# Projection matmuls of the tokens dealt by whole groups of 24 in every second round of the delta stage

## The chip, the core and the metric

One core of one Trainium2 chip runs the whole program. The metric is device time in microseconds (us), the median of several executions. Engines: TensorE (PE) for matmuls and transposes, VectorE (DVE), ScalarE (ACT), GpSimd (POOL), and SyncE (SP), which issues the DMAs. All engines run their own instruction streams in order and meet at semaphores.

## What is computed

Two transformer blocks in a row, float32, 1024 tokens of width 1024. The change touches one stage of the first block, "delta". With `xn` the normalised input, this stage computes a gated delta rule over 4 heads of 128 channels in chunks of 64 tokens, from projections made by the stage before:

```
kk = k k^T ; m = strict_lower(beta * kk * decay)
sol = solve(I + m, [beta v, beta k exp(gc)])  -> u, w
for each chunk: v_new = u - w state
                o     = q_dec state + (q k^T * decay) v_new
                state = state * g_end + k_dec^T v_new
```

and beside it an independent product, `xn` times 2560 more columns of `w_in` (the gate of this branch and q, k, v, z of the next). That product is "the tokens' projection", and is needed only in the next stage.

## The kernel before, in words

The program is a row of phases (`open`, `delta`, `stick`, `trunk`, `ffn`) with a barrier of all engines between them. In each phase several stage objects have one generator per engine. `interleave` (L2538) goes through a list of numbers, the plan, and for each number lets that generator issue its instructions up to its next `yield`. Each engine walks the same plan, so the plan sets the order within every engine; semaphores set the rest. A generator's first call also issues what stands before its loop.

In `delta` there are four: `DeltaFront` (0), `DeltaBack` (1), `DeltaScan` (2) and `TokenProjection` (3). The plan of `delta_plan` (L1387) has 144 rounds: 4 opening rounds, then 14 rounds (s = 0 to 13) for each of t = 0 to 9. In tile period t the front works on tile t (t = 0 to 7), the back on tile t - 1 (t = 1 to 8), the scan on tile t - 2 (t = 2 to 9). A tile has 128 tokens.

- Front: transposes `q`, `k`, `v` in rounds 0, 1, 2 (L1013), decay rows in round 3 (L1032), transposes of `kn`, `kb`, `qn`, `qd` in 6 to 9 (L1013), products `kk` (L1053) and `qk_dot` (L1058) in 10 and 11. DVE makes `kn`, `kb` in round 5 (L927, L931). ACT copies `qd`'s transpose to `q_t` in round 9 (L883), for which it waits for `o_done` of the tile two before, as `q_t` has two buffers.
- Back: inverts a triangular matrix in five levels. Round 0: DVE makes `upper` (L1100, L1102), PE transposes it (L1141). For level 1 to 5: in the odd round s = 1, 3, 5, 7, 9 PE multiplies `bx` (L1150) and ACT copies it (L1085); in the next even round PE multiplies `update` (L1157 and L1158, 16 instructions) and DVE subtracts it into `lower` and `upper` (L1106, L1107), which the next `bx` waits for. Rounds 11 and 12: `u_dot` (L1164), `w_dot` (L1169), and DVE's copy of the latter (L1111).
- Scan: in rounds 1 and 7 `ws` and the first half of `o` (L1250, L1255), in rounds 3 and 9 `grow` and the second half of `o` (L1263, L1267, signalling `o_done`).
- Tokens' projection: 80 groups (10 chunks of 256 columns by 8 token tiles) of 24 matmuls (L1379 to L1381), each group in two steps of 12; so 160 steps and two that only store. Even groups are evicted by ACT (L1353), odd ones by DVE (L1365), in the second step. Weights are split into a rounded high and a low part by ACT (L1328) and DVE (L1333); the first chunk's split is issued by the generator's first call.

The opening rounds make the gates: 48 matmuls of a narrow projection (L993 to L995), its copies (L828), transposes (L1000), DVE's L893, then beta, exp and log on ACT (L832, L833, L836, L838), sums over tokens on PE (L1006) and four exponentials on ACT (L841, L842, L844). PE waits for these before the first transposes of the tile loop (L1013).

The semaphore between groups and evictions, and two accumulators:

```python
            if h == 0 and g >= 2:
                pe.wait_ge(self.copied[g % 2], g // 2)
```

Of the kernel before, what the change touches and what calls it, by code (L numbers as in the profile page):

```python
# [1386 lines left out]
def delta_plan(others):  # L1387


    plan, given = [], 0  # L1390
    rounds = Delta.OPENING + Delta.STEPS * (TT + 2)
    for i in range(rounds):
        t = (i - Delta.OPENING) // Delta.STEPS if i >= Delta.OPENING else -1
        if t < TT:
            plan.append(0)
        if 1 <= t <= TT:
            plan.append(1)
        if t >= 2:
            plan.append(2)
        want = others * (i + 1) // rounds  # L1400
        plan += [3] * (want - given)
        given = want
    return plan


# [3210 lines left out]
```

## Time and profile before

| | |
|---|---|
| median of 3 executions | 2792.08 us (2791.32 to 2796.21) |
| the profiled execution | 2794.54 us, its span 2792.8 us |
| PE busy | 2614.5 us, 94% |
| DVE, ACT, POOL busy | 1263.7, 938.2, 357.3 us |
| delta stage on PE | first matmul 180.28, first of the projection 196.08, last about 681 us |
| projection matmuls L1379, L1380, L1381 | 640 each |
| PE waits in the stage that the list of waits shows | L1141 for `upper`: 4.3 us in 7 times; L1379 for `w_lo`: 2.9 us once |

In the timeline each row is a run of one instruction: its start, its length with the tail that overlaps the next, and in brackets the engine's idle time before it and who ended it. PE's matmuls are pipelined, so the time a block holds PE is read from its start to the start of the next block. A float32 product of 4 heads shows as 8 instructions, a transpose of 4 heads as 4.

### The profile page before, as it was taken

The numbers are of one execution on the slowest core, as the hardware profiler recorded it, in microseconds if no ns is written. First come the engines' busy times: TensorE is split into PE (matmuls) and PEld (weight loads), VectorE is DVE, ScalarE is ACT, GpSimd is POOL, SyncE is SP. The second block draws the span as 40 slices with busy tenths as digits, with TensorE's granted clock in tenths as the row PEclk, the third lists the DMA queues.
The fourth block names the chain that finished last, engine by engine and source line by source line (L and its number), as shares of the span: only waits on it lengthen the run. The fifth ranks groups of instructions, "written<-read, shape, count | busy, mean of one in ns | idle before, by whom it ended". The sixth has DMA issues, their size and how long they took to land. (4 is left out here: it accounts for less than half of the span.)

```text
span 2792.8 us, 36573 instructions
## 1 busy us (share of the span) xinstructions
PE 2614.5 (94%) x14702; PEld 2246.8 (80%) x14702; DVE 1263.7 (45%) x1762; ACT 938.2 (34%) x1541; POOL 357.3 (13%) x450
## 2 busy tenths in 40 slices
PE   8969999997799998999996989979999999999999
PEld 6849999997688886888885777868888888878877
DVE  6523444442466754543225767554323332333452
ACT  4223222221455652122114767532111211222331
POOL 1002222220332310001012223011000000000000
PEclk9989999999799998999997999989999999999999
DMA  4222221112332215442343111063222222255532
GB/s 144 86 77 80 62 68 52 52 41 68 106 113 88 80 50 192 155 143 82 121 135 119 46 39 47 18 222 89 83 68 68 68 83 76 91 189 176 192 102 80
DMA packets 223712, 268.91 MB, mean 96 GB/s; under 512 B 55060, under 2 KB 154004, under 8 KB 223544
## 3 DMA queue, kind: packets, MB, share of 16 engines
q1 hardware_dynamic: 223544, 266.58, 30.0%
q8 instruction: 117, 1.92, 0.3%
q14 instruction: 51, 0.42, 0.0%
HBM read 187.21 MB, written 79.32 MB: 95 GB/s over the span
## 5 line engine op out<-in xcount | busy, mean ns | idle before, releaser
L3784 PE MATMUL ffn_up_acc<-mixed_hi,ffn_ring_hi 128*128 128x512 f32 x704 | 274.6, 390 | 2.5 <-DVE mixed_lo L2926 2.5
L3784 PE MATMUL ffn_up_acc<-mixed_hi,ffn_ring_lo 128*128 128x512 f32 x704 | 274.3, 390 | 0.0
L3784 PE MATMUL ffn_up_acc<-mixed_lo,ffn_ring_hi 128*128 128x512 f32 x704 | 274.2, 389 | 0.0
L1379 PE MATMUL delta_acc<-delta_w_hi,xn_hi 128*128 128x256 f32 x640 | 191.6, 299 | 2.9 <-DVE delta_w_lo L1333 2.9
L1381 PE MATMUL delta_acc<-delta_w_hi,xn_lo 128*128 128x256 f32 x640 | 181.3, 283 | 0.0
L1380 PE MATMUL delta_acc<-delta_w_lo,xn_hi 128*128 128x256 f32 x640 | 181.1, 283 | 0.0
L3784 PEld LDWEIGHTS ffn_up_acc<-mixed_hi,ffn_ring_hi 128*128 128x128 f32 x704 | 132.2, 188 | 30.0 <-issue 2.9
L3784 PEld LDWEIGHTS ffn_up_acc<-mixed_hi,ffn_ring_lo 128*128 128x128 f32 x704 | 132.2, 188 | 27.5
L3784 PEld LDWEIGHTS ffn_up_acc<-mixed_lo,ffn_ring_hi 128*128 128x128 f32 x704 | 132.3, 188 | 27.1
L4043 DVE TENSOR_TENSOR ffn_feed_lo<-ffn_feed_raw,ffn_feed_hi 128x1536 fp32r<-128x1536 f32 x44 | 77.4, 1759 | 146.2 <-ACT ffn_feed_hi L4035 146.2
L3754 DVE TENSOR_SCALAR ffn_conv<-ffn_padded,ffn_taps 128x1024 f32<-128x1024 f32 x22 | 16.6, 753 | 274.8 <-ACT ffn_padded L3735 274.8
L1379 PEld LDWEIGHTS delta_acc<-delta_w_hi,xn_hi 128*128 128x128 f32 x640 | 122.2, 191 | 8.9 <-issue 5.5
L426 DVE TENSOR_TENSOR_SCAN stick_keep<-stick_keep,stick_zero 128x127 f32<-128x127 f32 (+7 forms) x64 | 92.4, 1444 | 74.1 <-ACT stick_keep L378 73.4
L3735 ACT ACTIVATE ffn_padded<-ffn_up_acc 128x1024 f32<-128x1024 f32 x22 | 22.6, 1027 | 301.4 <-PE ffn_up_acc L3784 301.4
L1380 PEld LDWEIGHTS delta_acc<-delta_w_lo,xn_hi 128*128 128x128 f32 x640 | 122.2, 191 | 0.0
L1381 PEld LDWEIGHTS delta_acc<-delta_w_hi,xn_lo 128*128 128x128 f32 x640 | 121.9, 191 | 0.0
L4035 ACT ACTIVATE ffn_feed_hi<-ffn_feed_raw 128x1536 fp32r<-128x1536 f32 x44 | 65.4, 1487 | 158.9 <-PE ffn_up_acc L4111 158.9
L593 PE MATMUL stick_g_acc<-xn_hi,stick_g_hi 128*128 128x512 f32 x256 | 107.8, 421 | 9.3 <-DVE stick_g_lo L573 8.8
L4111 PE MATMUL ffn_up_acc<-ffn_feed_hi 128*128 128x512 f32 x352 | 108.7, 390 | 1.4 <-DVE ffn_emb L3897 1.4
L4111 PE MATMUL ffn_up_acc<-ffn_feed_hi,ffn_feed_lo 128*128 128x512 f32 x352 | 108.5, 390 | 0.0
L4111 PE MATMUL ffn_up_acc<-ffn_feed_lo,ffn_feed_hi 128*128 128x512 f32 x352 | 108.4, 390 | 0.0
L594 PE MATMUL stick_g_acc<-xn_lo,stick_g_hi 128*128 128x512 f32 x256 | 102.0, 399 | 0.0
(440 smaller groups left out, 6462.3 us busy)
## 6 DMA issues: line engine op xcount, KB each, us to landing
ffn_feed_raw<-in_w_down SPq DMA_DIRECT2D x44, 512.0 KB, 4.0
ffn_ring_raw<-in_w_gate SPq DMA_DIRECT2D x11, 1024.0 KB, 5.3
ffn_ring_raw<-in_w_up SPq DMA_DIRECT2D x11, 1024.0 KB, 5.8
scratch_act_t<-ffn_silu SPq DMA_DIRECT2D x22, 512.0 KB, 2.7
ffn_feed_raw<-scratch_act_t SPq DMA_DIRECT2D x44, 256.0 KB, 2.9
delta_w_raw<-in_w_in SPq DMA_DIRECT2D x20, 512.0 KB, 4.0
scratch_projected<-delta_out SPq DMA_DIRECT2D x80, 128.0 KB, 1.7
stick_g_raw<-in_w_in SPq DMA_DIRECT2D x16, 512.0 KB, 4.7
```

The source lines that it names most:

```text
L426: nc.vector.tensor_tensor_scan(back, back, self.zero[:].to_broadcast([P, n - 1]), 1.0, ALU.mult, ALU.add).then_inc(self.scanned, 1)
L593: nc.tensor.matmul(self.acc[:], w_hi, self.hi[:, k, cols], start=(k == 0), stop=False, skip_group_check=True)
L594: nc.tensor.matmul(self.acc[:], w_hi, self.lo[:, k, cols], start=False, stop=False, skip_group_check=True)
L1379: nc.tensor.matmul(acc, self.hi[:, k, tok], w_hi, start=(k == 0), stop=False, skip_group_check=True)
L1380: nc.tensor.matmul(acc, self.hi[:, k, tok], w_lo, start=False, stop=False, skip_group_check=True)
L1381: last = nc.tensor.matmul(acc, self.lo[:, k, tok], w_hi, start=False, stop=(k == self.kt - 1), skip_group_check=True)
L3735: nc.scalar.activation(self.padded[s][:, taps - 1:], self.acc[s][:, 0, :], ACT.Copy).then_inc(self.copied, 1)
L3754: nc.vector.tensor_scalar(self.conv[s][:], self.padded[s][:, 0:SEQ], self.taps_sb[:, f, 0:1], None, ALU.mult).then_inc(self.tapped, 1)
L3784: last = nc.tensor.matmul(self.acc[s][:, br, cols], weight[:, k, ch], part[:, k, cols], start=(k == 0 and first), stop=(k == 7 and weight ...
L4035: self.nc.scalar.activation(self.hi[s][:], self.raw[s][:], ACT.Copy).then_inc(self.hi_done[s], 1)
L4043: self.nc.vector.tensor_tensor(self.lo[s][:], self.raw[s][:], self.hi[s][:].bitcast(F32), ALU.subtract).then_inc(self.lo_done[s], 1)
L4111: last = nc.tensor.matmul(t.pairs[j][:, half, :], part, weight[:, HALF + half * HALF:HALF + (half + 1) * HALF], start=begins, stop=ends, s ...
```

## The change

```diff
@@ delta_plan @@
-        want = others * (i + 1) // rounds
-        plan += [3] * (want - given)
-        given = want
+        if i % 2 == Delta.OPENING % 2 or i == rounds - 1:
+            want = others * (i + 1) // rounds // 2 * 2
+            plan += [3] * (want - given)
+            given = want
```

`others` is 162 and `rounds` 144. Before, each round had one step of 12 matmuls, every eighth two. Now the steps stand in the even rounds of each tile period alone, two at a time (one group of 24), in some rounds four. The opening rounds 0 and 1 have none, round 2 has the first group, round 3 none. On PE the runs of projection matmuls without another instruction between them go from 121 to 68.

ACT in the opening rounds, from the copies of the narrow projection to the first exponentials (`delta_w_hi` is the high part of the projection's weights, `delta_out` the eviction of its first group). Before:

```order
L828 ACTIVATE delta_tok<-delta_back 8x512 x2
L1328 ACTIVATE delta_w_hi<-delta_w_raw 128x1024 x2
L832 ACT_TABLE_LOAD
L832 ACTIVATE delta_by_tile<-delta_ba 128x8x4
L833 ACT_TABLE_LOAD
L833 ACTIVATE delta_exp_a<-delta_a_row 128x4
L1353 ACTIVATE delta_out<-delta_acc 128x256
L836 ACTIVATE delta_expx<-delta_clip 128x32
L838 ACT_TABLE_LOAD
L838 ACTIVATE delta_rest<-delta_expx 128x32
L841 ACT_TABLE_LOAD
L841 ACTIVATE delta_by_tile<-delta_by_tile 128x8x4
```

And now:

```order
L828 ACTIVATE delta_tok<-delta_back 8x512 x2
L832 ACT_TABLE_LOAD
L832 ACTIVATE delta_by_tile<-delta_ba 128x8x4
L833 ACT_TABLE_LOAD
L833 ACTIVATE delta_exp_a<-delta_a_row 128x4
L836 ACTIVATE delta_expx<-delta_clip 128x32
L838 ACT_TABLE_LOAD
L838 ACTIVATE delta_rest<-delta_expx 128x32
L1328 ACTIVATE delta_w_hi<-delta_w_raw 128x1024 x2
L1353 ACTIVATE delta_out<-delta_acc 128x256
L841 ACT_TABLE_LOAD
L841 ACTIVATE delta_by_tile<-delta_by_tile 128x8x4
```

The split of the first weights and the first eviction move behind the logarithm.

PE in rounds 9 and 10 of a tile period with all three stages: `qd` transposed, `bx`, the two products of the scan, then what follows. Before:

```order
L1013 MATMUL delta_front<-ident,delta_qd 128x128 x4
L1150 MATMUL delta_back<-delta_lower,delta_bt 128x128 x4
L1263 MATMUL delta_ws<-delta_v_new,delta_k_end 128x128 x4
L1267 MATMUL delta_o_acc<-delta_v_new,delta_qk_t 64x128 x4
L1379 MATMUL delta_acc<-delta_w_hi,xn_hi 128x256
L1380 MATMUL delta_acc<-delta_w_lo,xn_hi 128x256
L1381 MATMUL delta_acc<-delta_w_hi,xn_lo 128x256
```

And now:

```order
L1013 MATMUL delta_front<-ident,delta_qd 128x128 x4
L1150 MATMUL delta_back<-delta_lower,delta_bt 128x128 x4
L1263 MATMUL delta_ws<-delta_v_new,delta_k_end 128x128 x4
L1267 MATMUL delta_o_acc<-delta_v_new,delta_qk_t 64x128 x4
L1053 MATMUL delta_front<-delta_t_sb 128x128 x4
L1157 MATMUL delta_back<-delta_bx,delta_upper 128x128
L1158 MATMUL delta_back<-delta_upper,delta_bx 128x128
```

Half a group stood between the scan's L1267 and the front's L1053; now L1053 and `update` follow directly.

DVE in rounds 3 to 6 of the same tile period (L1365 evicts a group, L927 makes `kn`). Before:

```order
L1237 TENSOR_TENSOR delta_state<-delta_faded,delta_ws 128x512
L1365 COPY delta_out<-delta_acc 128x256
L1106 TENSOR_TENSOR delta_lower<-delta_lower,delta_back 128x512
L1107 TENSOR_TENSOR delta_upper<-delta_upper,delta_back 128x512
L1333 TENSOR_TENSOR delta_w_lo<-delta_w_raw,delta_w_hi 128x1024
L927 TENSOR_TENSOR delta_kn<-delta_tok,delta_norm 128x512
L931 TENSOR_TENSOR delta_kb<-delta_kn,delta_by_tile 128x512
```

And now:

```order
L1237 TENSOR_TENSOR delta_state<-delta_faded,delta_ws 128x512
L1106 TENSOR_TENSOR delta_lower<-delta_lower,delta_back 128x512
L1107 TENSOR_TENSOR delta_upper<-delta_upper,delta_back 128x512
L1365 COPY delta_out<-delta_acc 128x256
L927 TENSOR_TENSOR delta_kn<-delta_tok,delta_norm 128x512
L931 TENSOR_TENSOR delta_kb<-delta_kn,delta_by_tile 128x512
L934 TENSOR_TENSOR delta_qn<-delta_tok,delta_norm 128x512
```

The eviction moves from before `lower` and `upper` to between them and `kn`, and the split of weights L1333 leaves this place.

## Rows read from the trace of the kernel before

**Rows 1.** Busy us by stretch: PE, PEld, DVE, ACT, POOL; then PEclk, DMA, GB/s

```profile
300.00:400.00 100.00, 99.39 (x838) 96.00 (x837) 44.76 (x64) 26.99 (x46) 22.92 (x19) 1.00 0.21 59
```

**Rows 2.** Timeline of PE, tile t = 4: start, length, instruction

```profile
400.19 1.05 PE L1032 MATMUL delta_front<-chunk_upto,delta_gb 128*128 128x128 f32 x8
...
401.32 1.13 PE L1150 MATMUL delta_back<-delta_lower,delta_bt 128*128 128x128 f32 x8
...
404.48 0.39 PE L1379 MATMUL delta_acc<-delta_w_hi,xn_hi 128*128 128x256 f32 x1
...
407.41 0.38 PE L1157 MATMUL delta_back<-delta_bx,delta_upper 128*128 128x128 f32 x2
...
409.11 0.36 PE L1379 MATMUL delta_acc<-delta_w_hi,xn_hi 128*128 128x256 f32 x1
...
410.82 1.13 PE L1150 MATMUL delta_back<-delta_lower,delta_bt 128*128 128x128 f32 x8
...
411.71 0.36 PE L1379 MATMUL delta_acc<-delta_w_hi,xn_hi 128*128 128x256 f32 x1
...
413.21 0.60 PE L1013 MATMUL delta_front<-ident,delta_kn 128*128 128x128 f32 x4
...
413.65 0.39 PE L1157 MATMUL delta_back<-delta_bx,delta_upper 128*128 128x128 f32 x2
```

**Rows 3.** Timeline of PE, tile t = 0

```profile
210.43 0.60 PE L1013 MATMUL delta_front<-ident,delta_xt 128*128 128x128 f32 x4
...
210.79 0.36 PE L1379 MATMUL delta_acc<-delta_w_hi,xn_hi 128*128 128x256 f32 x1
```

**Rows 4.** Timeline of ACT, s = 5 of t = 4

```profile
411.99 0.60 ACT L1085 ACTIVATE delta_bx<-delta_back 128x512 f32<-128x512 f32 x1 [5.35 <-PE delta_back L1150]
```

**Rows 5.** Timeline of PE and ACT, s = 9 of t = 4

```profile
428.85 0.39 PE L1379 MATMUL delta_acc<-delta_w_hi,xn_hi 128*128 128x256 f32 x1
...
429.02 0.60 ACT L883 ACTIVATE delta_q_t<-delta_front 128x512 f32<-128x512 f32 x1 [6.09 <-PE delta_o_acc L1267]
...
429.51 0.59 ACT L1085 ACTIVATE delta_bx<-delta_back 128x512 f32<-128x512 f32 x1
```

**Rows 6.** Timeline of PE, the first products of back in t = 1 and 5

```profile
237.19 0.66 PE L1141 MATMUL delta_back<-ident,delta_upper 128*128 128x128 f32 x4 [1.41 <-DVE delta_upper L1102]
...
443.63 0.66 PE L1141 MATMUL delta_back<-ident,delta_upper 128*128 128x128 f32 x4 [0.20 <-DVE delta_upper L1102]
```

**Rows 7.** Timeline of ACT, the opening rounds

```profile
193.73 1.99 ACT L1328 ACTIVATE delta_w_hi<-delta_w_raw 128x1024 fp32r<-128x1024 f32 x2
...
201.70 0.38 ACT L1353 ACTIVATE delta_out<-delta_acc 128x256 f32<-128x256 f32 x1 [0.85 <-PE delta_acc L1381]
...
203.52 0.23 ACT L838 ACTIVATE delta_rest<-delta_expx 128x32 f32<-128x32 f32 x1
...
203.76 1.28 ACT L841 ACT_TABLE_LOAD   x1
...
206.11 0.26 ACT L844 ACTIVATE delta_chunk_decay<-delta_o_acc 128x32 f32<-128x32 f32 x2
```

**Rows 8.** Timeline of PE, the opening rounds

```profile
196.08 0.39 PE L1379 MATMUL delta_acc<-delta_w_hi,xn_hi 128*128 128x256 f32 x1 [2.88 <-DVE delta_w_lo L1333]
...
197.79 1.02 PE L1000 MATMUL delta_ws<-ident,delta_tok 8*128 8x8 f32 x8
...
198.74 0.58 PE L1379 MATMUL delta_acc<-delta_w_hi,xn_hi 128*128 128x256 f32 x1
...
204.25 0.45 PE L1006 MATMUL delta_o_acc<-delta_g,chunk_upto 128*128 128x32 f32 x2
...
206.72 0.49 PE L1013 MATMUL delta_front<-ident,delta_xt 128*128 128x128 f32 x3
```

**Rows 9.** Busy time by stretches, columns as in rows 1

```profile
197.00:198.00 1.00, 1.00 (x9) 0.78 (x8) 0.16 (x1) 0.02 (x1) 0.00 (x0) 0.77 0.67 121
...
204.00:205.00 1.00, 0.98 (x9) 0.75 (x7) 0.19 (x1) 1.00 (x1) 0.00 (x0) 0.81 0.00 0
```

## The prediction

> **What bounds the kernel.** The stage is fenced by a barrier on either side, so only its own length counts. I read first the busy time by stretches: in the middle of the stage TensorE (PE) is busy 99.4% at the full clock (1.00, its 2.4 GHz level), VectorE (DVE) 45% and ScalarE (ACT) 27% [rows 1]. So the stage is as long as PE's work plus PE's waits; the change removes no matmul, and can only alter waits, the price of changing between kinds of matmul, and the clock.
>
> The list of waits shows few, since its ends are modelled; so I read the timeline and took start to start. Twelve projection matmuls take 1.50 (411.71 to 413.21), twenty-four 2.93 (404.48 to 407.41) [rows 2]: 1.43 for the second twelve, so entering a visit costs 0.08 us. But four transposes take 0.44 before another short product (413.21 to 413.65, [rows 2]) and 0.36 before a visit (210.43 to 210.79, [rows 3]): the short block gives the 0.08 back. **A visit of the projection is free at both ends**, and 121 visits becoming 68 (53 fewer, 1920 matmuls in both) earns nothing by itself.
>
> **What the new order takes away.** (a) Level 2's `bx` product (s = 3) now waits for DVE: L1032 took 1.13 before it (400.19 to 401.32) where eight such instructions take 0.89 (as 410.82 to 411.71) [rows 2]. A whole group ahead of it at s = 2 covers the missing 0.24: seven tiles (t = 1 to 7), -1.7 us. (b) At s = 4 a half group took 1.71 in place of 1.50 before `bx` (409.11 to 410.82), waiting for `upper` [rows 2]. Eleven places read so: s = 4 of seven tiles, and four in t = 8. All get 24 matmuls of cover: 11 times 0.21, -2.3. Together **-4.0**.
>
> **What it adds in the bare rounds.** The odd rounds have no projection now. Even to odd nothing is lost: 2.93 of cover stands where 1.50 did. Odd to even the chain is `bx` on PE, its copy on ACT (L1085), `update` on PE. The copy starts 1.17 after `bx` starts (410.82 to 411.99) and takes 0.60 [rows 2, 4]; the handover to PE is not shown for ACT, and I bound it by 0.05 and 0.15 and take 0.05 to 0.1: `update` can start 1.85 after `bx`. PE has 0.89 of `bx` itself, and then:
> - s = 5 to 6: only the four transposes of `kn`, 0.44: wait 0.5. On DVE the eviction L1365 of an odd group (s = 4 always has one in t = 1 to 7) now stands before `kn` (L927); group end + 0.2 + 0.33 + 0.69 + 0.1 = 1.3 lets the transposes begin 0.4 late, which lies inside the same 0.5. Seven tiles: 3.5.
> - t = 1 has no scan: s = 1 to 2 and s = 7 to 8 have 0.44 of transposes each (0.5 each), s = 3 to 4 has nothing (0.95). t = 8 has no front: s = 5 to 6, 0.95. Together 2.9.
> - s = 9 to 10, t = 2 to 7: ACT is in order, and `q_kept` (L883) ahead of the `bx` copy waits for the scan's `o_done` of this very round. The copy starts 0.66 after the scan leaves PE (428.85 to 429.51) and ends at 1.25 [rows 5]; `update` at 1.35, where PE has L1053, 0.89: 0.45 each, 2.7.
> - s = 1 to 2, 3 to 4 and 7 to 8 of t = 2 to 7: two scan products, some 1.9 to 2.1, cover 0.96. Nothing. s = 11 to 12: `w_dot` waits for an old `wr`. Nothing.
>
> Sum **+9.1**; bounds 7 (handover 0.05, and the order helps) and 11 (handover 0.15, 0.1 more at each).
>
> **Tile boundaries.** `upper0` (L1100, L1102) must be done before L1141. Where DVE evicts an odd group last before it, the wait shows as 1.41 (237.19), else as 0.20 (443.63) [rows 6]: 1.2 more. Before, that was so entering t = 1 and 2. By the new numbering the group at s = 12 is 8, 16, 24, 32, 40, 47, 55, 63: odd entering t = 6, 7 and 8. One more, +1.2; plain waits of 0.4 go at two boundaries (t = 1 and t = 5) and come at one: **+0.8**.
>
> **The opening.** The plan no longer calls the projection in rounds 0 and 1. Its two halving copies (L1328, 2 us on ACT) and subtractions (L1333) are the first thing its generator issues, so they move behind the logarithm L838 (the order shows it). Before: L1328 at 193.73, first projection matmul at 196.08, so 2.35 later [rows 7, 8]. After: PE's L1000 can go at 193.9 instead of 197.79. Behind it the chain to L838 took 5.73 (197.79 to 203.52, [rows 7, 8]), with 1.1 in it for an eviction in ACT's way that now comes later (0.85 of idle before L1353 and 0.28 to the next [rows 7]): L838 at 198.5, L1328 at 198.75, first projection matmul at **201.1**. PE idles 6 us, and the clock is down: before, it fell at about 197.8 after 3 idle us and came back near 204.4 [rows 9], and 24 matmuls took 5.5 (198.74 to 204.25) [rows 8]. I take 4.5 to 5.3 for the first group (end 205.6 to 206.4). Then L1006, waiting for nothing; ACT evicts the group, 0.6, loads its table (L841, 1.28) and does four exponentials, 0.5 [rows 7], before L1013 may start: 2.45 after L1006, so 208.1 to 208.9, against 206.72 [rows 8]. And 24 instead of 48 projection matmuls are done by then: 24 times 0.118 = 2.8 owed. Late by 4.2 to 5.0; taken **+4.5**. Bounds: 2.6 (the first group at the full clock) and 8.3 (the 2 us idle after L1006 brings a second cold spell like the first: 6.6 us at half speed, 3.3 lost). t = 0 itself has whole groups in plenty and no back chain: nothing. What is stored and loaded by SP keeps two to three groups of slack: a group is evicted, and stored two groups later, as before; nothing.
>
> **Sum:** -4.0 + 9.1 + 0.8 + 4.5 = **+10.4 us**. The profiled execution took 2794.54, which gives 2804.9; it stands 2.46 above the median of the three runs (2792.08), so the median forecast is **2802.5 us**.
>
> **Rule against row.** In the stretch of rows 1 PE stood for 0.2 us at several places a tile and the granted clock stayed at 1.00. I therefore charge the new waits of half a microsecond at their length alone. The Trainium skill, "TensorE: Matmul & The Clock Gate", section "A second HAM failure mode: psum-queue depth-cycling", says that TensorE standing briefly and often between groups of matmuls makes its clock fall and rise again and again. By that rule the sum would be larger by the third rival's amount; the trace so far disagrees with it.
>
> **Rivals.**
> 1. *Not slower: changing kinds costs more than the rows show.* Place: the 53 visits that go. Most direct neighbours now created (L1267 to L1157, L1255 to L1013, L1150 to L1013) never stood together, and L1267 and L1255 before a visit read 0.1 long. If each removed visit returned 0.08 (its entry, not given back by the short block), -4.2, so 2798. From 0.2 each the whole loss is paid and the time is 2792. For: the entry of 0.08 is plain. Against: the 0.44 and 0.36 above. Chance 0.13 for some of it, 0.05 for the full price.
> 2. *The waits of the bare rounds hide*: the copy reaches PE sooner than I think, or a wait at s = 5 delays DVE's and ACT's next work so that the next cover is richer. Then only the opening, the boundaries and half the waits stay: 2792.1 - 4.0 + 4.5 + 0.8 + 4.6 = 2798. Against: each wait is a pure chain from PE over ACT to PE. Chance 0.10.
> 3. *The clock.* A second cold spell in the opening: +3.3, so 2806. One in each of eight tiles: 8 times 3.3 over the forecast, 2829. For: the opening has two gaps now. Against: rows 1. Chance 0.12 and 0.02.
> 4. *The change does nothing*: excluded by the order; both engines' rows move.
>
> **Numbers.** The forecast as argued has 0.58. What can be told from no change is about 0.2%, 5.6 us: 2786.5 to 2797.7. Range **2795 to 2811**: below, rival 2 and the partial rival 1 less 3 us of error in the opening; above, a second cold spell, and waits at their upper bound (+2). It leaves out the full rival 1 and the clock in every tile, and my own errors of counting. Faster needs 0.3 us from each of the 53 visits, or several terms wrong at once: 0.04. Same: the full rival 1 (0.05) and about half of the partial rival 1 and of rival 2, which lie on the bound (0.12): 0.17. Slower: the rest, 0.79.
>
> **What would show it.** In the profile after: L1000 near 194, first L1379 near 201, L1013 first at 208 to 209; the pairs `bx` to `update` 1.8 to 1.9 apart at s = 5 and the scan to `update` 1.35 at s = 9; L1032 before `bx` 0.89; L1141 waiting 1.4 and more entering t = 6, 7, 8; a visit of 24 at 2.93 and a direct pair of short blocks at 0.11 us per instruction. Wrong would be: direct neighbours cheaper than that, `update` without a wait at s = 6 and s = 10, or PE's first projection before 198.

## The result, and the profile after

The kernel before took 2791.56 us (median of 8 runs, 2789.92 to 2796.21), the changed one **2803.44 us** (median of 8, 2800.38 to 2812.93): 11.9 us more. The ratio is 1.0044, with a 95% interval of 1.0032 to 1.0055, so the change made the kernel slower, by 9 to 15 us. The forecast was 2802.5.

| | before | after |
|---|---|---|
| profiled execution, us | 2794.54 | 2801.49 |
| its span, us | 2792.8 | 2799.7 |
| PE busy, us | 2614.5 | 2610.1 |
| last narrow matmul (L995) to the last scan product (L1267) | 481.13 | 491.47 |
| last narrow matmul to the last projection matmul | 487.80 | 498.15 |

The last two lines are read from the timeline and are the length of the stage that the change touches, without what other stages do in an execution. I call the first of the two **the stage** and use it for all runs; where a plan moves projection matmuls behind the last scan product, the second says what was really gained, and is given too. The stage grew by **10.3 us** in the profiled executions. The spans differ by less, 6.9, and the medians by 11.9: one execution differs from the next by some microseconds elsewhere, which the change does not reach. The same kernel once more (last experiment) gave a stage of 491.64.

Busy time by stretches of the kernel after, columns as in [rows 1], for the middle of the stage and then microsecond by microsecond through the opening:

```profile
300.00:400.00 100.00, 98.45 (x829) 94.86 (x828) 42.97 (x61) 26.11 (x47) 22.91 (x19) 1.00 0.20 55
...
196.00:197.00 1.00, 0.00 (x0) 0.00 (x0) 0.00 (x0) 0.99 (x3) 0.00 (x0) 0.50 0.00 0
...
205.00:206.00 1.00, 0.00 (x0) 0.00 (x0) 0.17 (x1) 0.99 (x5) 0.00 (x0) 1.00 0.39 132
206.00:207.00 1.00, 0.80 (x5) 0.80 (x5) 0.00 (x0) 0.67 (x3) 0.00 (x0) 0.52 0.00 0
207.00:208.00 1.00, 1.00 (x7) 1.00 (x6) 0.00 (x0) 0.60 (x1) 0.00 (x0) 0.50 0.00 0
...
210.00:211.00 1.00, 1.00 (x10) 1.00 (x10) 0.00 (x0) 0.00 (x0) 0.00 (x0) 1.00 0.00 0
```

PE lost one busy microsecond in a hundred in the middle (99.39 in [rows 1], 98.45 now) at the same clock, and in the opening the granted clock is down twice, once from the time that PE stands before the first group until into that group, and again from 206 on, after PE had stood through 205.

The opening on PE and on ACT, which answers to [rows 7] and [rows 8]:

```profile
192.42 0.66 PE L1000 MATMUL delta_ws<-ident,delta_tok 8*128 8x8 f32 x8 [0.68 <-ACT delta_tok L828]
199.34 0.58 PE L1379 MATMUL delta_acc<-delta_w_hi,xn_hi 128*128 128x256 f32 x1 [6.26 <-DVE delta_w_lo L1333]
...
203.74 0.30 PE L1006 MATMUL delta_o_acc<-delta_g,chunk_upto 128*128 128x32 f32 x2
...
206.20 1.12 PE L1013 MATMUL delta_front<-ident,delta_xt 128*128 128x128 f32 x4 [1.49 <-ACT delta_chunk_decay L844]
206.97 0.56 PE L1379 MATMUL delta_acc<-delta_w_hi,xn_hi 128*128 128x256 f32 x1
...
211.00 1.04 PE L1013 MATMUL delta_front<-ident,delta_xt 128*128 128x128 f32 x8
```

```profile
196.85 0.23 ACT L838 ACTIVATE delta_rest<-delta_expx 128x32 f32<-128x32 f32 x1
196.99 1.99 ACT L1328 ACTIVATE delta_w_hi<-delta_w_raw 128x1024 fp32r<-128x1024 f32 x2
...
203.94 0.38 ACT L1353 ACTIVATE delta_out<-delta_acc 128x256 f32<-128x256 f32 x1 [4.96 <-PE delta_acc L1381]
204.34 1.28 ACT L841 ACT_TABLE_LOAD   x1
```

The halving copy now stands behind the logarithm, as the order of the instructions said; PE waits 6.26 for the projection's first weights (2.88 in [rows 8]). The first twenty-four matmuls take 4.40 (199.34 to 203.74), the next twenty-four 4.03 (206.97 to 211.00), both with the granted clock at 0.50 for part of the time; 2.93 is the length at the full clock.

Tile t = 4 on PE, which answers to [rows 2] and [rows 5]:

```profile
403.89 1.05 PE L1032 MATMUL delta_front<-chunk_upto,delta_gb 128*128 128x128 f32 x8
404.78 1.06 PE L1150 MATMUL delta_back<-delta_lower,delta_bt 128*128 128x128 f32 x8
...
409.68 0.36 PE L1379 MATMUL delta_acc<-delta_w_hi,xn_hi 128*128 128x256 f32 x1
...
412.60 1.05 PE L1150 MATMUL delta_back<-delta_lower,delta_bt 128*128 128x128 f32 x8
413.97 0.63 PE L1013 MATMUL delta_front<-ident,delta_kn 128*128 128x128 f32 x4 [0.32 <-DVE delta_kn L927]
414.44 0.40 PE L1157 MATMUL delta_back<-delta_bx,delta_upper 128*128 128x128 f32 x2
...
431.02 1.16 PE L1053 MATMUL delta_front<-delta_t_sb 128*128 128x128 f32 x8
432.33 0.49 PE L1157 MATMUL delta_back<-delta_bx,delta_upper 128*128 128x128 f32 x2
```

Both removed waits are gone: `bx` starts 0.89 after L1032 (1.13 in [rows 2]), and the group at s = 4 takes 2.92 up to its `bx` (409.68 to 412.60). Both added waits are there. At s = 5 `bx` to the transposes is 1.37, where eight such instructions take 0.89: 0.48 of wait. At s = 9 L1053 to `update` is 1.31: 0.42. The engines beside the first of them:

```profile
412.80 0.42 DVE L1365 COPY delta_out<-delta_acc 128x256 f32<-128x256 f32 x1 [1.56 <-PE delta_acc L1381]
413.14 0.68 DVE L927 TENSOR_TENSOR delta_kn<-delta_tok,delta_norm 128x512 f32<-128x512 f32 x1
```

```profile
413.69 0.60 ACT L1085 ACTIVATE delta_bx<-delta_back 128x512 f32<-128x512 f32 x1 [4.61 <-PE delta_back L1150]
```

DVE's eviction pushes `kn` to 413.82, and PE's transposes wait for it; the copy of `bx` ends at 414.29, and `update` follows at 414.44 without a wait of its own. So the two waits that the prediction laid on top of each other do lie on top of each other.

The first product of back, entering t = 4 and t = 6 to 8, which answers to [rows 6]:

```profile
392.12 0.66 PE L1141 MATMUL delta_back<-ident,delta_upper 128*128 128x128 f32 x4 [0.33 <-DVE delta_upper L1102]
...
498.66 0.66 PE L1141 MATMUL delta_back<-ident,delta_upper 128*128 128x128 f32 x4 [1.82 <-DVE delta_upper L1102]
554.35 0.66 PE L1141 MATMUL delta_back<-ident,delta_upper 128*128 128x128 f32 x4 [1.83 <-DVE delta_upper L1102]
610.06 0.66 PE L1141 MATMUL delta_back<-ident,delta_upper 128*128 128x128 f32 x4 [2.26 <-DVE delta_upper L1102]
```

The long wait came at the three boundaries foretold, 0.4 longer than it was entering t = 1 and 2 before.

### The profile page after: what moved, and what is told of

It reads as the page before. It is cut to its first block and busy times, and to the rows that moved or that the text cites. A ratio compares the mean times of both kernels' runs of the same rounds, so it can differ in the third digit from the quotient of the medians.

```text
span 2799.7 us, 36573 instructions
## 1 busy us (share of the span) xinstructions
PE 2610.1 (93%) x14702; PEld 2242.9 (80%) x14702; DVE 1261.2 (45%) x1762; ACT 936.9 (33%) x1541; POOL 356.5 (13%) x450
```

## The experiments

Every count of a stage below is one profiled execution, and the opening alone differs between executions: from the last narrow matmul to the first L1141 it took 45.28, 45.48, 45.48 and 46.42 us in four executions with the changed kernel's opening. Every ratio is over several runs with its interval. The theory: waits have prices, given by what work stands between `bx` and `update`, by who evicts ahead of L1141, and by when the projection starts. The first rival: the number of visits is what counts.

### The opening, alone and undone

The changed kernel with one projection step in each opening round:

```diff
-        if i % 2 == Delta.OPENING % 2 or i == rounds - 1:
+        if i < Delta.OPENING:
+            plan.append(3)
+            given += 1
+        elif i % 2 == Delta.OPENING % 2 or i == rounds - 1:
```

> The stage is measured from PE's last narrow matmul (L995) to its last L1267: 481.1 us in the kernel before, 491.5 in the changed one. This kernel deals whole groups as the changed one, but gives each of the four opening rounds one step, as before. Waits theory: the part from the last narrow matmul to the first L1013 is 13.9 again, no cold spell follows, and the stage falls by 5.3 to about 486.2; whole kernel about 2797 to 2799. Theory that visits cost: the opening is no part of the loss, the stage stays above 489. Clock theory: the clock in the later tiles was lower after the opening, more than 6 comes back.

And the kernel before with its first two projection steps held back to round 2, all else as it was:

```diff
-        want = others * (i + 1) // rounds
-        plan += [3] * (want - given)
-        given = want
+        if i >= Delta.OPENING or i == 2:
+            want = others * (i + 1) // rounds if i > 2 else 2
+            plan += [3] * (want - given)
+            given = want
```

> The kernel before, with the projection kept out of opening rounds 0, 1 and 3 and two steps in round 2, everything later dealt by halves as before. Waits theory: the opening alone costs 5.3, the stage is 486.4 against 481.1 and the first L1013 comes 14.9 after the last narrow matmul with 24 projection matmuls done. A rival says that the debt of 24 matmuls is made up in tile 0, where PE could have slack: then the stage is 483.5 or less.

The first: 2799.02 us, ratio 1.0025 (1.0012 to 1.0037); L1013 at +12.92 after the last narrow matmul (+14.85 in the changed kernel), and every tile began 5.1 earlier. Its opening was not quite the one expected (L1013 at 13.9, the clock up): behind the same 2.88 us wait as before, the clock stayed up at first (1.00 from 197 to 198, 0.77 in [rows 9]), and it fell later, behind a wait of 1.45 at L1006:

```profile
205.00:208.00 3.00, 3.00 (x16) 2.77 (x16) 0.42 (x1) 1.37 (x3) 0.00 (x0) 0.50 0.00 0
```

At the end only 3.6 of the 5.1 was left: stage 487.90. The missing 1.5 is in one place, the group behind the 2.25 us wait entering t = 8, in the busy time by stretches:

```profile
606.00:608.00 2.00, 1.56 (x11) 1.56 (x12) 0.39 (x1) 0.60 (x1) 0.00 (x0) 0.86 0.00 0
608.00:610.00 2.00, 2.00 (x12) 2.00 (x11) 0.00 (x0) 0.00 (x0) 0.00 (x0) 0.50 0.00 0
```

The granted clock fell to half after that wait and 24 matmuls took 4.44; in two executions of the changed kernel the clock stayed at 1.00 after the same wait. The second: 2798.51, ratio 1.0017 (1.0008 to 1.0027), stage 486.78, which is 5.7 more than before; its L1013 is at +15.12:

```profile
207.91 1.00 PE L1013 MATMUL delta_front<-ident,delta_xt 128*128 128x128 f32 x4 [1.49 <-ACT delta_chunk_decay L844]
```

So **the opening costs 5.1 to 5.7 us**, taken away or put in alone, each in one execution.

### The evictions

The changed kernel with all of the projection's evictions on ACT:

```diff
-            if h == 1 and g % 2 == 0:
+            if h == 1:
                 self.wait_sum(act, g)
-                self.nc.scalar.activation(self.out_sb[g % 4][:], self.acc[0][:, 0:self.width], ACT.Copy).then_inc(self.copied[0], 1)
+                self.nc.scalar.activation(self.out_sb[g % 4][:], self.acc[g % 2][:, 0:self.width], ACT.Copy
+                                          ).then_inc(self.copied[g % 2], 1)
...
-            if h == 1 and g % 2 == 1:
-                self.wait_sum(dve, g)
-                self.nc.vector.tensor_copy(self.out_sb[g % 4][:], self.acc[1][:, 0:self.width]).then_inc(self.copied[1], 1)
```

> The changed kernel with every eviction on ACT, so that DVE has none before L1100 and L927. Waits theory: the idle before L1141 entering t = 6, 7, 8 falls from 1.8, 1.8, 2.3 to 0.3, 0.3, 0.7, so -4.6; at s = 5 to 6 the chain over ACT takes the place of DVE's, and only 0.05 to 0.1 of 0.48 goes. Stage 486.4. Rival: DVE's eviction is what costs at s = 5, then a further 3 us go, stage 483.5. Rival: ACT becomes late with its copies, stage no shorter than 489.

Ratio 1.0025 (1.0014 to 1.0036). L1141 now waits 0.30, 0.30 and 0.77 entering t = 6, 7 and 8 (1.82, 1.83, 2.26 in the changed kernel); the first and the last:

```profile
500.08 0.66 PE L1141 MATMUL delta_back<-ident,delta_upper 128*128 128x128 f32 x4 [0.30 <-DVE delta_upper L1102]
...
608.45 0.66 PE L1141 MATMUL delta_back<-ident,delta_upper 128*128 128x128 f32 x4 [0.77 <-DVE delta_upper L1102]
```

From the start of t = 1 to that of t = 8 the timeline measures 368.9 in place of 373.4: 4.5 less, as expected. The stage came out at 488.06 (486.4 expected), since its opening was 1.1 longer in this execution. At s = 5, where DVE has no eviction ahead of `kn` any more, the time to `update` is 0.41 too long in place of 0.48, and a tile without a long wait is no shorter (54.19 against 54.20 from the L1141 of t = 2 to that of t = 3): the chain over ACT costs about the same there. So DVE's eviction of an odd group right ahead of `upper0` costs 1.5 at each of the three boundaries.

### The bare rounds

The changed kernel with the groups of s = 4 and s = 8 split, their second half in the round behind, so that both chains over ACT are covered again:

```diff
             want = others * (i + 1) // rounds // 2 * 2
-            plan += [3] * (want - given)
-            given = want
+            held = 1 if i > Delta.OPENING and s in (4, 8) and want > given else 0
+            plan += [3] * (want - given - held)
+            given = want - held
+        elif i > Delta.OPENING and s in (5, 9) and given % 2:
+            plan.append(3)
+            given += 1
```

> The changed kernel, but the group of rounds s = 4 and s = 8 is split again, one half in the even round and one in the odd round behind it, so that bx to update has 12 matmuls of cover at s = 5 and s = 9. 17 more visits (85 against 68). Waits theory: the waits of 0.48 (seven tiles), 0.95 (t = 8) and 0.42 plus 0.1 (six tiles) go, the 0.21 at s = 4 comes back in seven tiles: -5.9 at best, -5 with small changes, stage 485.6 to 486.5. Theory that visits cost 0.1 each: +1.7, so 487.5 or more. If nothing changes, the waits were not what the time went to.

The stage is 485.48, **6.0 less**, with 85 visits in place of 68. Of this 1.4 is no gain: 12 more projection matmuls stand behind the last scan product, and to the last projection matmul it is 493.58 in place of 498.15, **4.6 less**. By the rows the waits at s = 5 and 9 that went are 6.7, and the 0.21 that came back at s = 4 is 1.7 in eight places: 5.0. In t = 4 `bx` takes its 0.88, twelve matmuls follow, and the transposes come without a wait:

```profile
410.76 1.13 PE L1150 MATMUL delta_back<-delta_lower,delta_bt 128*128 128x128 f32 x8
411.64 0.37 PE L1379 MATMUL delta_acc<-delta_w_hi,xn_hi 128*128 128x256 f32 x1
...
413.15 0.60 PE L1013 MATMUL delta_front<-ident,delta_kn 128*128 128x128 f32 x4
```

The five runs of the whole kernel scatter from 2793.89 to 2808.21 (median 2801.95, ratio 1.0035, 1.002 to 1.0049), so the whole does not show the gain; the stage of the one profiled execution does. More visits and less time is what the waits say, and the opposite of what the visits say.

### The price of a visit

The kernel before with each projection step made of 6 matmuls and twice as many steps, dealt between the front's and the back's work and behind the scan's: 191 visits in place of 121.

```diff
             for k in range(h * kp, (h + 1) * kp):
+                if k == h * kp + kp // 2:
+                    yield
...
+        want = others * (i + 1) // rounds
         if t < TT:
             plan.append(0)
+        plan += [3] * (want - given)
...
-        want = others * (i + 1) // rounds
```

> The kernel before, with each step of 12 projection matmuls dealt as 6 behind the front's work and 6 at the end of the round: the same matmuls in 191 visits in place of 121, with the same cover between each producer and its consumer to within 6 matmuls. Waits theory, by which a visit is free: the stage (last narrow matmul to last L1267) stays 481.1, within 1.5. Theory that a visit costs its entry of 0.08: +5.6, 486.7. Theory that it costs 0.2 in all, which would have paid for the change: +14, 495.

Ratio 0.9988 (0.9978 to 0.9998), stage 477.45: 3.7 less than before (4.4 to the last projection matmul), with 70 more visits. The timeline shows the give-back again: four transposes between two visits take 0.36 (389.03 to 389.39). That refutes a price that decides: at 0.2 a visit the stage would have grown by 14. But the stage was to stay within 1.5 of 481.1, and did not, as the cover moved more than was thought. The two kernels are level where t = 1 begins (44.44 and 44.39 after the last narrow matmul). From there on the waits of 0.24 ahead of the `bx` of s = 3 are gone in all seven tiles (1.7), the wait of 1.41 entering t = 2 is 0.69 (0.7), and three of the eleven waits of 0.21 are gone (0.6). That is 3.0 of the 3.7, and the more than 60 visits added there cost nothing that can be seen. The kernel is a test of the visits only with these waits counted.

### Whole groups in the odd rounds

The changed kernel with the groups in the odd rounds, one step in each opening round:

```diff
-        if i % 2 == Delta.OPENING % 2 or i == rounds - 1:
+        if i < Delta.OPENING:
+            plan.append(3)
+            given += 1
+        elif i % 2 == 1:
```

> Whole groups, as in the changed kernel with its opening rounds served as before, but in the odd rounds. 68 visits, as many as in the changed kernel. Waits theory: bx to update is covered now, update to the next bx is bare. That chain takes 1.71 over DVE (at s = 2 to 3 some 4.2 from the v transposes), against 0 to 0.9 of other work: about 1.6 + 1.7 + 1.3 + 1.3 + 0.8 = 6.7 in each of seven tiles, 8 in t = 8, and 9 of bare bx waits gone: stage near 532. Theory by which the number of visits sets the time: 486, as with whole groups in the even rounds.

One execution: 2855.83 us, stage 539.98, **58.9 more than before with the same 68 visits as the change**. Its even rounds have no projection, so the `bx` of the next odd round waits for DVE's `upper` after `update`; L1150 in t = 5:

```profile
484.40 0.79 PE L1150 MATMUL delta_back<-delta_lower,delta_bt 128*128 128x128 f32 x5 [1.49 <-DVE delta_upper L1107]
...
493.91 1.13 PE L1150 MATMUL delta_back<-delta_lower,delta_bt 128*128 128x128 f32 x8 [1.47 <-DVE delta_upper L1107]
...
504.41 0.79 PE L1150 MATMUL delta_back<-delta_lower,delta_bt 128*128 128x128 f32 x5 [1.03 <-DVE delta_upper L1107]
```

The next L1141 starts 60.6 later (472.31 to 532.87), where the kernel before takes 53.5 for the same tile. In two of the tiles, t = 3 and t = 7, the granted clock fell as well, for 6.8 us each, with PE standing several times for 1.0 to 1.5 us in every tile; the first:

```profile
365.00:371.00 6.00, 6.00 (x28) 5.45 (x27) 0.69 (x1) 1.11 (x2) 1.54 (x2) 0.50 0.18 46
```

These two tiles took 63.6 against 60.6, so some 6 of the 58.9 are the clock's, and most of what the expected 532 lacked. So the choice of the even rounds, not the number of visits, is what keeps the changed kernel close to the kernel before.

### A plan by the waits: four tries

If waits have prices, a plan that puts projection matmuls where they are should beat both kernels. First, a second half group in s = 2, 4 and 12, the even rounds of t = 8 filled, all evictions on ACT:

```diff
-        want = others * (i + 1) // rounds
-        plan += [3] * (want - given)
-        given = want
+        count = 1
+        if 1 <= t < TT and s in (2, 4, 12):
+            count = 2
+        if t == TT and s in (2, 4, 6, 8, 10):
+            count = 2
+        if t == TT + 1:
+            count = 1 if s in (1, 3, 5, 7, 9, 11) else 0
+        if i == rounds - 1:
+            count = others - given
+        plan += [3] * count
+        given += count
```

> A version made from the theory: half groups in each round as before, the 18 spare steps and eight taken from t = 9 put at s = 2, 4 and 12 of t = 1 to 7 and s = 2 to 10 of t = 8, and all evictions on ACT. Waits theory: the 0.24 and 0.21 waits (4.0) and those before L1141 (5.7) go; the later of PE's last L1267 and last projection matmul comes 9 to 10 sooner than the 487.8 of the kernel before, about 478.5; whole kernel 0.3% to 0.35% faster. Rival: ACT, with 40 more evictions, becomes late, and less than half of it is seen.

A miss: ratio 0.9995 (0.9985 to 1.0005), stage to the last projection matmul 484.68, to the last scan product 485.98, so 1.8 less than the 487.80 of the kernel before, where 9 to 10 were expected. The rows of L1141 show where it went:

```profile
389.25 0.66 PE L1141 MATMUL delta_back<-ident,delta_upper 128*128 128x128 f32 x4 [2.14 <-DVE delta_upper L1102]
445.17 0.66 PE L1141 MATMUL delta_back<-ident,delta_upper 128*128 128x128 f32 x4 [1.46 <-DVE delta_upper L1102]
...
611.48 0.66 PE L1141 MATMUL delta_back<-ident,delta_upper 128*128 128x128 f32 x4 [2.58 <-DVE delta_upper L1102]
```

With 17 steps in a tile and 16 in a chunk of weights, the split of the next weights (a half of it takes 1.05 on ACT, L1328, and 1.22 on DVE, L1333) wanders through the tile's rounds, and came to stand just ahead of `upper0`: entering t = 4, L1333 starts at 386.64 and L1100 right behind it at 387.78. The long waits of L1141 name DVE; whether ACT's added evictions have a part in the miss was not separated.

Second, the same with a fifth opening round, the weight split issued ahead of the copies of the narrow projection (a bare yield ahead of the other generators' first work), and half groups 1, 2, 3, 1 in the opening, none in s = 11 to 13 of t = 0:

```diff
-    H, LEVELS, STEPS, OPENING = 4, 5, 14, 4
+    H, LEVELS, STEPS, OPENING = 4, 5, 14, 5
...
+        yield
...
-        count = 1
+        count = (1, 1, 2, 3, 1)[i] if t < 0 else 1
+        if t == 0 and s in (11, 12, 13):
+            count = 0
```

> As the version before it, and the first chunk's weights are split on ACT and DVE before the copies of the narrow projection (an extra opening round makes room), with seven steps in the opening and none at s = 11 to 13 of t = 0. Theory: PE's 2.9 us of idle behind the narrow matmuls goes, and with it the spell at half the clock behind it (24 matmuls in 5.5 in place of 2.93): 5 more than the placed version, about 473.5, 0.5% faster than the kernel before. Rival: the chain of table loads on ACT (about 6 us from L1000 to L1006) bounds the opening, and only 2 or 3 come.

Ratio 0.998 (0.9969 to 0.999), 479.45 to the last projection matmul and 480.74 to the last scan product: not the 473.5 expected, as the first try's miss stayed in it, but 5.2 less than the first try, where 5 was expected, with every tile 5.2 earlier. The rival, that the table loads leave only 2 or 3, is refuted. Third, half groups from a table with exactly 16 steps a tile, on the kernel before, with its evictions and its opening; fourth, the same table with the early opening (the text put on record calls the second try `placed_early` and the third `place16`):

```diff
+        row = {-1: (1, 1, 1, 1), TT: (1, 0, 2, 0, 2, 1, 2, 0, 2, 0, 2, 0, 1, 1)}.get(t, (1,) * 14)
+        if 1 <= t < TT:
+            row = (1, 1, 2, 1, 2, 1, 1, 1, 1, 1, 1, 0, 2, 1)
+        if t == TT + 1:
+            row = (1, 1, 1, 1, 1, 2, 1, 1, 1, 1, 1, 1, 1, 4)
+        count = row[i if t < 0 else s]
```

> The kernel before with the 160 half groups dealt by a table: the opening and t=0 one per round as before; in t=1 to 7 two in s=2, 4 and 12, none in s=11, one elsewhere (16 per tile, so that the weight split and the vector engine's evictions keep the same rounds in every tile); in t=8 two in s=2, 4, 6, 8, 10, none in s=1, 3, 7, 9, 11; the rest in t=9. Waits have prices: the bare even rounds of t=8 gain 5.5, the second half groups at s=2, 4 and 12 gain 2.3, and no odd group is evicted by the vector engine ahead of L1141, which gains 1.7: stage 471.6 (before 481.1), last projection matmul +478.3 (before +487.8), whole ratio 0.9965. Only the count of half groups matters: 1.000. If the vector engine's queue again grows somewhere, waits before L1141 of over 1 us show at those tiles.

> The same table with the early start of placed_early: weight split ahead of the copies of the narrow projection, half groups 1, 2, 3, 1 in the opening, none at s=1, 7 and 9 of t=0. Waits and cover add up: another 5 below place16, last projection matmul +473.5, last L1267 466.5, whole ratio 0.9945. If the two gains share their cause (work moved to the same places), it comes out as place16 or placed_early.

Third: 2785.99 us, ratio **0.997** (0.996 to 0.998); to the last scan product 470.85 (471.6 expected). Fourth: 2777.64 us, ratio **0.9945** (0.993 to 0.996); to the last scan product 464.13 (466.5 expected). To the last projection matmul they are 480.37 and 473.66, against 478.3 and 473.5 expected. That is the gain to go by, 7.4 and 14.1, since 24 more projection matmuls stand behind the last scan product than in the kernel before; the third fell 2.1 short of what was expected, and the early opening gave 6.7 between the two, where 5 was expected. L1141 shows a wait only entering t = 8, and from t = 2 on starts every 53.2 us. The third:

```profile
383.52 0.66 PE L1141 MATMUL delta_back<-ident,delta_upper 128*128 128x128 f32 x4
436.71 0.66 PE L1141 MATMUL delta_back<-ident,delta_upper 128*128 128x128 f32 x4
...
596.30 0.65 PE L1141 MATMUL delta_back<-ident,delta_upper 128*128 128x128 f32 x4 [0.59 <-DVE delta_upper L1102]
```

In the fourth the granted clock stays at 1.00 behind the narrow matmuls, where PE has matmuls from 0.23 after the last of them; its busy time by stretches:

```profile
195.00:200.00 5.00, 5.00 (x46) 4.84 (x46) 0.79 (x4) 4.57 (x9) 0.00 (x0) 1.00 0.09 30
200.00:205.00 5.00, 5.00 (x45) 5.00 (x44) 2.23 (x6) 2.56 (x5) 0.00 (x0) 1.00 0.15 52
```

### The changed kernel again

> The changed kernel once more, in the same call. If the second spell of the low clock behind the opening belongs to the change (its wait of some 1.5 us at L1013), its records show it again and the stage is 491.5 +-1; if it is chance, the granted clock of the stretch is 1.00 and the stage is 490.1. Ratio to the kernel before 1.0044.

Ratio 1.004 (1.0026 to 1.0054), stage 491.64 (491.47 the first time). The second fall of the clock came again:

```profile
207.00:208.00 1.00, 0.27 (x2) 0.27 (x3) 0.00 (x0) 0.99 (x6) 0.00 (x0) 0.86 0.12 39
208.00:209.00 1.00, 1.00 (x6) 1.00 (x6) 0.00 (x0) 0.31 (x2) 0.00 (x0) 0.50 0.00 0
```

It stands as well in the three other kernels that start the projection late (the kernel before with its opening held back, the changed one with all evictions on ACT, and the one with split groups). So it belongs to the change that the clock falls twice in the opening. With the opening of before it falls once, and in two ways: behind the 2.88 us wait and for 6.8 us in three kernels (the one before, and the first and third of the four tries), or later and for 3.4 us, behind a wait of 1.45, in three others (the changed one with the early opening, the steps of 6 matmuls, the odd rounds). What decides between the two was not tried.

## Why the prediction was right, and where its terms were not

The forecast (10.4 us; 2802.5) met the stage (10.3) and the median (2803.44), but two terms are too small, one is too large and one is missing, and they happen to cancel. The mechanism held (waits uncovered in the bare rounds, at the boundaries and in the opening); that the sum came within 0.1 is luck, as single terms are off by 0.7 to 1.8. The measured terms are read from the rows of one execution each.

| term | predicted | measured |
|---|---|---|
| removed waits at s = 2 to 3 and s = 4 | -4.0 | -4.0 |
| bare rounds | +9.1 | +8.4 |
| tile boundaries | +0.8 | +2.5 |
| opening | +4.5 | +5.2 |
| visits and their neighbours | 0 | -1.8, as remainder |
| stage | +10.4 | +10.3 |

**Removed waits.** As the rows of t = 4 show: 0.24 and 0.21, at the places counted.

**Bare rounds.** s = 5 to 6: 0.48 in seven tiles, 3.4 (0.5 each was said). The wait at L1013 is for DVE's `kn`, which the eviction delays, and hides the one for the copy; either alone gives about the same, as the run without DVE's evictions has 0.41 there. s = 9 to 10: 0.42 six times, 2.5 (2.7). In t = 1: 0.41, 0.85, 0.41, 1.7; in t = 8: 0.85; together 2.5 (2.9). The forecast had `update` 1.85 after `bx`, the rows of t = 1 have 1.74. Refilling s = 5 and s = 9 gave 4.6 back, where the rows say 5.0.

**Boundaries.** The rule (an odd group last ahead of L1141) and the three tiles were right; the price was not. "1.2 more" was taken from the boundary into t = 1, where L1100 took 0.68 and POOL had nothing to do. At the boundaries into t = 6 and 7 L1100 takes 1.10 beside POOL's L1121, and the wait is 1.82; into t = 8, where it had been 0.66, it is 2.26. Summed over all boundaries the waits of L1141 are 6.86 after and 4.33 before: +2.5. The eviction experiment took 4.5 of the 6.86 away.

**Opening.** Counted from the last narrow matmul (at 192.80 before, 191.35 after), L1013 came at +14.85, 0.9 later than before; I had said 15.3 to 16.1, with the first group 0.3 later than it came (+7.99) and slower than the 4.40 it took. The 24 matmuls owed are 2.8, as said. The second fall of the clock adds 1.1 in the next group (4.03 for 2.93) and some 0.35 in L1013 ahead of it: 5.2 in all. The forecast had that fall as a case of its own, chance 0.12 and 3.3 us; it came in every execution seen with this opening, at less than half the price, since it lasted 3.4 us, where 6.6 had been taken from the first (by [rows 9] rather 6.8: 0.77 of the stretch from 197 puts the fall at 197.5, not 197.8). L1013 as a mark of the opening is good to about 1 us only: in two executions with the projection dealt early as before, it came 0.9 and 1.0 earlier than in the profile of the kernel before, and t = 1 began no earlier.

**Visits.** "A visit of the projection is free at both ends" is nearly right: as a price that decides, the visit is refuted, since 70 more of them cost nothing that can be seen. But a short block gives 0.08 back only where it is a transpose or a product of front or back. The scan's products take as long ahead of a visit as ahead of another block (L1255 0.96 both ways), so at four places of a tile a removed visit saves its 0.08; what pays most of it back is `update`, 1.81 in place of 1.70 straight behind a scan product and behind the wait of s = 9. In t = 3, over like stretches of the two timelines, projection blocks are 0.6 shorter apart from the 0.21 of s = 4, and 0.4 comes back at their neighbours. That is worked out from rows, not isolated by a run; the -1.8 of the table is what the other lines leave over.

**The rule on the clock.** I had charged the new waits of half a microsecond at their length alone, against what the Trainium skill says in "TensorE: Matmul & The Clock Gate", section "A second HAM failure mode: psum-queue depth-cycling", of short repeated pauses. In the middle of the stage the granted clock stayed at 1.00 with waits of 0.3 to 1.8 us, some each tile: the trace disagrees with the rule, and the sum without it was the right one. The odd rounds are nearer to the rule: there, with waits of 1.0 to 1.5 us several times a tile, the clock fell in two tiles of eight. In all these kernels it fell only behind single waits of 1.4 us and more, and behind few of those.

**The rivals.** Visits that cost: refuted by 70 more of them and by the odd rounds. Waits that hide: refuted, 8.4 of 9.1 came. The clock in every tile: refuted; the second spell in the opening: came, smaller.

## What to carry to other kernels

Where one engine is nearly always busy, count not how often it changes its kind of work but which chains over other engines have too little of its work between their two ends; cover is worth 0.2 to 0.95 us per place here, and a visit nothing measurable. Put filler by place (a table of rounds), with a count per tile that keeps slow side work, such as an eviction or a weight split, in the same rounds of every tile. (The first and third try differ in this, but also in who evicts; the rows of L1333 speak for the count.) And look first at what the filler's first call issues: moving that by two rounds cost more here than any other single place.

## What the runs showed that was not expected

- The clock fell behind a wait of 1.49 us in the opening, in both executions of the changed kernel, and behind one of 1.45 in three others; behind a wait of 2.25 entering t = 8 it fell in one kernel and not in the changed one, where the projection around it was the same. What makes the difference was not tried.
- DVE's product of 128x512 with two operands in SBUF (L1100) takes 0.68 alone and 1.10 when it starts while POOL runs one of its own; a copy from PSUM does not show it, nor does an operation with one operand in PSUM (L1107, 0.68 beside POOL too). POOL and DVE entering t = 6 of the changed kernel:

```profile
494.81 2.52 POOL L1121 TENSOR_TENSOR delta_bt<-delta_mt,delta_mask 128x512 f32<-128x512 f32 x2
```

```profile
496.44 0.43 DVE L1365 COPY delta_out<-delta_acc 128x256 f32<-128x256 f32 x1 [2.14 <-PE delta_acc L1381]
496.78 1.10 DVE L1100 TENSOR_TENSOR delta_upper<-delta_mt,delta_mask 128x512 f32<-128x512 f32 x1
497.91 0.69 DVE L1102 TENSOR_TENSOR delta_upper<-ident,delta_upper 128x512 f32<-128x512 f32 x1
```

  POOL's pair ends at 497.33 and L1100 0.55 later, nearly its whole length alone; L1102 starts with POOL done and takes 0.69. Entering t = 2 POOL's work reaches further, and L1102 is slow as well:

```profile
282.01 1.66 DVE L1102 TENSOR_TENSOR delta_upper<-ident,delta_upper 128x512 f32<-128x512 f32 x1
```

  It ends 0.54 after POOL's first L1121 (283.13). The Trainium skill, "SBUF — State Buffer", section "Who interferes with whom", says that a DVE instruction with two inputs in SBUF contends with a POOL instruction that reads SBUF, over a pair of ports that is an exclusive lock. The trace agrees, and the forecast had left it out.

- Smaller pieces of filler (6 matmuls) were a little better than 12, with no plan of places at all: 0.9988, its interval ending at 0.9998. Most of the 3.7 us are waits that went by themselves, as counted under that experiment: those ahead of the `bx` of s = 3, and 0.7 of the one entering t = 2.
